# Gates of the first block by seven products of token sums, with one weight sum per attention step

## What is computed

```python
h = rmsnorm(x, norm_attn) * (1 + scale) + shift
qa, ka, va, qb, kb, vb, ga, gb = split(h @ w_in)    # ga, gb: 1024 columns each
ya = gqa_attend(qa, ka, va)                         # 8 heads, 512 wide
yb = rmsnorm(diff_attend(qb, kb, vb, lam), subln)   # 4 heads of 128
merged = sigmoid(ga) * (ya @ w_oa) + sigmoid(gb) * (yb @ w_ob)
x = x + g_a * (merged @ w_out)
x = x + g_m * moe(modulated rmsnorm(x))             # 32 experts, 4 per token
```

## Time and profile before

| | us |
|---|---|
| median of 3 runs | 1747.19 (1745.96 to 1748.6) |
| profiled execution | 1749.62 |
| its span | 1747.8 |
| PE busy | 1635.1 (94%) |
| DVE, ACT busy | 730.3 (42%), 277.9 (16%) |
| mean granted clock of PE | 0.99 |

### The profile page before, as it was taken

How to read it: one execution, slowest core, us unless ns; L and a number is a source line. 1 busy time by engine, 2 the same in 40 slices (tenths; PEclk the granted TensorE clock), 3 DMA queues, 4 the chain that set the end, 5 groups by cost and what they waited for, 6 DMA issues and landing times.

```text
span 1747.8 us, 18802 instructions
## 1 busy us (share of the span) xinstructions
PE 1635.1 (94%) x7152; PEld 873.7 (50%) x7152; DVE 730.3 (42%) x1327; ACT 277.9 (16%) x611; POOL 25.1 (1%) x30
## 2 busy tenths in 40 slices
PE   5999999999989798898897988998999999999998
PEld 3567786533333242333332423333686776688754
DVE  2796432333314223233142233233234663677755
ACT  3123440301010010100100100000243333010000
POOL 0210000000000000000000000000000000000000
PEclk9999999999999999999999999999999999999999
DMA  9796236899999999999999999999733334454440
GB/s 381 277 338 192 94 112 238 336 429 429 429 430 429 429 431 428 430 430 429 431 429 429 431 428 430 431 427 421 257 110 131 114 141 144 145 188 150 158 179 24
DMA packets 86685, 537.18 MB, mean 307 GB/s; under 512 B 6208, under 2 KB 7616, under 8 KB 60512
## 3 DMA queue, kind: packets, MB, share of 16 engines
q1 hardware_dynamic: 82816, 530.60, 74.8%
q10 hardware_dynamic: 3808, 5.78, 0.9%
HBM read 535.31 MB, written 1.05 MB: 307 GB/s over the span
## 4 chain that ended last, share of the span: by engine, by line
PE 67%; DMA 25%; DVE 5%; DVEq 1%; issue 1%; POOL 0%; ACT 0%; SPq 0%; POOLq 0%
PE ps L2398 22%; PE ps L1986 21%; DMA ring<-in_w_up 14%; DMA ring<-in_w_gate 10%; PE ps L2750 6%; PE ps L2980 4%; PE ps L2368 3%; PE ps L2460 2%; DVE arena L1167 2%; DMA ring<-in_w_ada 2%; PE ps L2865 1%; PE ps L2972 1%; PE ps L2249 1%; PE ps L2200 0%; PE ps L2196 0%
## 5 line engine op out<-in xcount | busy, mean ns | idle before, releaser
L2398 PE MATMUL ps<-ring,arena 128*64 128x512 f32 x2288 | 513.5, 597 | 51.5 <-DMA ring<-in_w_gate 23.1
L2398 PEld LDWEIGHTS ps<-ring,arena 128*64 128x64 f32 x2288 | 160.8, 137 | 386.1 <-issue 314.5
L2398 PE MATMUL ps<-arena 128*64 128x512 f32 x784 | 178.8, 601 | 10.1 <-DMA arena<-in_w_up 5.6
L1986 PE MATMUL ps<-ring,arena 128*128 128x512 f32 (+1 forms) x528 | 183.1, 502 | 0.3 <-issue 0.3
L1986 PE MATMUL ps<-arena,ring 128*128 128x256 f32 x704 | 158.2, 382 | 0.3 <-ACT arena L805 0.3
L1986 PEld LDWEIGHTS ps<-arena,ring 128*128 128x128 f32 x704 | 131.9, 190 | 28.2 <-issue 6.8
L1986 PEld LDWEIGHTS ps<-ring,arena 128*128 128x128 f32 x528 | 99.3, 190 | 74.5 <-issue 68.1
L877 ACT ACTIVATE arena<-ps 128x512 f32<-128x512 f32 x32 | 19.1, 597 | 670.6 <-PE ps L2438 670.6
L2398 PEld LDWEIGHTS ps<-arena 128*64 128x64 f32 x784 | 56.1, 138 | 117.8 <-issue 101.8
L1457 DVE TENSOR_TENSOR arena<-ps,arena 128x512 f32<-128x512 f32 x32 | 22.1, 692 | 202.2 <-PE ps L2398 202.2
L1482 DVE TENSOR_TENSOR arena<-ps,g_moe 64x512 f32<-64x512 f32 x32 | 21.9, 683 | 185.6 <-PE ps L2398 185.6
(11 more groups left out here) (361 smaller groups left out, 1591.1 us busy)
## 6 DMA issues: line engine op xcount, KB each, us to landing
ring<-in_w_up SPq DMA_DIRECT2D x54, 2048.0 KB, 33.8
ring<-in_w_down SPq DMA_DIRECT2D x53, 2048.0 KB, 31.8
ring<-in_w_gate SPq DMA_DIRECT2D x47, 2048.0 KB, 33.6
ring<-in_w_in SPq DMA_DIRECT2D x23, 2048.0 KB, 9.1
arena<-in_w_down SPq DMA_DIRECT2D x17, 2048.0 KB, 32.0
arena<-in_w_up SPq DMA_DIRECT2D x16, 2048.0 KB, 30.5
arena<-in_w_gate SPq DMA_DIRECT2D x15, 2048.0 KB, 30.8
ring<-in_w_ada SPq DMA_DIRECT2D x12, 2048.0 KB, 17.3
```

The costliest lines, as they stand in the source:

```text
L1986: last = pe.matmul(dst, a, b, start=k == 0, stop=k == len(terms) - 1)
L2398: mm = pe.matmul(dst[CAP * g:CAP * g + CAP, :], stationary(half, c), w[:, c, 512 * g:512 * g + 512], start=half == 0 and c == 0, stop=half ...
```

## The change

- **Gates.** Each gate block `u` (0 to 3, 512 columns) is made by seven products of four 128x256 multiplies (`gate_product`), with tokens stationary and weight blocks or their sums moving; 28 products instead of 16 halves of eight. The token sums are those of the value projection, which keep their place; the transposed probabilities move to another for that. Products 1, 6, 5, 3 go to bank 7 and are copied by ACT, 256 columns each (16 copies instead of 8 of 512). 2, 7, 4 go to bank 5, and DVE adds each (`gate_add`, 12 adds).
- **Weight sums.** DVE makes four per block (`gate_sum`), at most one per step. The first stands between the last two value adds, before the loop. One of their two places is the stretch of `const` where the routing constants stood; their load (576 KB) moves from the start of ACT's program to behind the loop.
- **Transposes.** Bank 5 being taken, all go to bank 4, and those of step k wait for ACT's copy of step k - 1.
- **Merge.** Gates are now token by column. So `branch_product` has tokens stationary (32 multiplies of 512 columns), `merged` is token by column, and PE transposes it (`merged_turn`, twice eight pieces), ACT copying the result to `mergedT` in four pieces.
- **Sigmoids.** Four of 1024 columns instead of eight of 512.
- **Router weights.** The eight small loads by ACT stand one per step in steps 17 to 24, instead of two per step in 18 to 21, and their place in memory is another.

```diff
@@ -202,9 +203,38 @@
             return k if k < 16 else 16 + 2 * (k - 16)
-        def gate_fill(k):
-            return 8 + k - 16 if 16 <= k < 24 else k // 2 if k < 16 and k % 2 == 0 else None
+        GATE_FILL = {0: ((0, 1), (0, 2)), 2: ((0, 7),), 3: ((0, 6),), 4: ((0, 5),), 5: ((0, 3),), 6: ((0, 4),),
...
+        GATE_MADE = [g for k in sorted(GATE_FILL) for g in GATE_FILL[k]]
+        GATE_SUMS = {1: (0, 1), 2: (0, 2), 3: (0, 4), 5: (1, 3), 6: (1, 1), 7: (1, 2), 9: (1, 4), 11: (2, 3), 12: (2, 1),
...
+        GATE_ADDS = {1: (0, 2), 5: (0, 7), 7: (0, 4), 9: (1, 2), 12: (1, 7), 14: (1, 4), 16: (2, 2), 18: (2, 7), 19: (2, 4),
...
+        gate_t2 = const[:, P:P + 1024].rearrange("p (j c) -> p j c", j=4)
+        gate_t3 = area(20480, 1024).rearrange("p (j c) -> p j c", j=4)
+        def gate_quarter(u, n):
+            tile, half = {1: (0, 0), 2: (0, 0), 6: (1, 0), 4: (1, 0), 5: (1, 1), 7: (1, 1), 3: (0, 1)}[n]
+            return sig[:, u, tile, T * half:T * half + T]
...
...
@@ -699,7 +729,6 @@
...
                                    bias=modT[:, j, m:m + 1]).then_inc(sem("ht_act"), 1)
-            act.dma_start(const[:, P:C_ROPEC], t["const"][:, P:C_ROPEC]).then_inc(sem("const_in"), 16)
...
@@ -799,28 +828,38 @@
...
                     pt_out(k)
-                if gate_fill(k) is not None and gate_fill(k) % 2 == 1:
-                    s = gate_fill(k) // 2
-                    act.wait_ge(sem("gate_done"), s + 1)
-                    act.activation(sig[:, s, :], bank(7), ACT.Copy).then_inc(sem("gate_read"), 1)
+                for u, n in GATE_FILL.get(k, ()):
+                    if n in (1, 6, 5, 3):
+                        act.wait_ge(sem("gate_done"), gate_number(u, n))
+                        if k == 16:
+                            act.wait_ge(sem("pv_done"), 4)
+                        act.activation(gate_quarter(u, n), bank(7, T), ACT.Copy).then_inc(sem("gate_read"), 1)
...
                     pv_out(4 + k - 1 - 16)
-                if 18 <= k < 22:
-                    a = k - 18
-                    for h in range(2):
+                if 17 <= k < 25:
+                    a = (k - 17) // 2
+                    for h in ((k - 17) % 2,):
...
                                       ).then_inc(sem("rw_in"), 16)
+            act.dma_start(const[:, P:C_ROPEC], t["const"][:, P:C_ROPEC]).then_inc(sem("const_in"), 16)
             act.drain()
-            for s in range(8):
-                act.activation(sig[:, s, :], sig[:, s, :], ACT.Sigmoid).then_inc(sem("sig_ready"), 1)
+            for u in range(4):
+                g = sig[:, u].rearrange("p t n -> p (t n)")
+                act.wait_ge(sem("vb_added"), gate_added(u, 4))
+                act.activation(g, g, ACT.Sigmoid).then_inc(sem("sig_ready"), 1)
...
                                scale=sub08).then_inc(sem("ybt_read"), 1)
+            for q in range(4):
+                tt, half = q // 2, q % 2
+                act.wait_ge(sem("ybt_done"), 2 + q + 1)
+                act.activation(mergedT[:, 4 * half:4 * half + 4, P * tt:P * tt + P],
+                               bank(4 + q).rearrange("p (j q) -> p j q", j=4), ACT.Copy).then_inc(sem("ybt_read"), 1)
...
@@ -1241,6 +1280,30 @@
...
                 dve.tensor_tensor(a, bank(2 * m + 1, T), a, ALU.add).then_inc(sem("vb_added"), 1)
+            def gate_sum(u, n):
+                w = wq_view(W_GATE + u)
+                b11, b12, b21, b22 = w[:, 0:4, 0:T], w[:, 0:4, T:2 * T], w[:, 4:8, 0:T], w[:, 4:8, T:2 * T]
+                if n == 3:
+                    i = W_GATE + u
+                    dve.wait_ge(loaded[i % RING], 16 * (i // RING + 1))
+                    if u:
+                        dve.wait_ge(sem("gate_done"), gate_number(u - 1, 7))
+                    else:
+                        dve.wait_ge(sem("qkt_done"), 12)
+                if n == 4:
+                    dve.wait_ge(sem("gate_done"), gate_number(u, 2))
...
+                a, b, c = {3: (gate_t3, b22, b12), 1: (b12, b12, b11), 2: (gate_t2, b22, b12), 4: (b21, b21, gate_t2)}[n]
+                dve.tensor_tensor(a, b, c, ALU.subtract).then_inc(sem("vb_sums"), 1)
+            def gate_add(u, n):
+                dve.wait_ge(sem("gate_done"), gate_number(u, n))
+                dve.wait_ge(sem("gate_read"), gate_copied(u, {2: 1, 7: 5, 4: 6}[n]))
+                a = gate_quarter(u, n)
+                dve.tensor_tensor(a, bank(5, T), a, ALU.add).then_inc(sem("vb_added"), 1)
...
@@ -1272,8 +1334,9 @@
...
             modulation_out(9)
-            for n, m in VB_SUMS[4:6]:
-                vb_add(n, m)
+            vb_add(*VB_SUMS[4])
+            gate_sum(0, 3)
+            vb_add(*VB_SUMS[5])
...
@@ -1324,22 +1387,30 @@
...
                     step_maxes(k + 2)
+                if k < 16 and k in GATE_ADDS:
+                    gate_add(*GATE_ADDS[k])
+                if k in GATE_SUMS:
+                    gate_sum(*GATE_SUMS[k])
+                if k >= 16 and k in GATE_ADDS:
+                    gate_add(*GATE_ADDS[k])
...
             dve.tensor_tensor(obuf, obuf, brs.unsqueeze(2).broadcast_to([P, 8, P]), ALU.mult).then_inc(sem("on_done"), 1)
+            def merged_part(s):
+                return merged[:, s // 2, 512 * (s % 2):512 * (s % 2) + 512]
             for s in range(4):
...
                 dve.wait_ge(sem("ta_done"), s + 1)
-                dve.tensor_tensor(mergedT[:, 2 * s:2 * s + 2, :].rearrange("p j q -> p (j q)"), bank(s),
-                                  sig[:, s, :], ALU.mult).then_inc(sem("ta_read"), 1)
+                dve.tensor_tensor(merged_part(s), bank(s), sig[:, s % 2, s // 2], ALU.mult).then_inc(sem("ta_read"), 1)
             for s in range(4):
...
-                m = mergedT[:, 2 * s:2 * s + 2, :].rearrange("p j q -> p (j q)")
...
+                m = merged_part(s)
...
@@ -2173,18 +2245,37 @@
...
                     qk_transpose(s - 2)
-            def gate_half(h):
-                s, c = h // 2, h % 2
-                i, c0 = W_GATE + s // 2, T * (s % 2) + P * c
-                if c == 0 and s:
-                    pe.wait_ge(sem("gate_read"), s)
-                ready(i)
-                w = wq_view(i)
-                last = product(bank(7)[:, T * c:T * c + T], [(w[:, j, c0:c0 + P], hT[:, j, 0:T]) for j in range(KC)])
-                if h % 4 == 3:
+            def gate_product(u, n):
+                w = wq_view(W_GATE + u)
+                b11, b12, b21, b22 = w[:, 0:4, 0:T], w[:, 0:4, T:2 * T], w[:, 4:8, 0:T], w[:, 4:8, T:2 * T]
+                j0, tile, source = {1: (0, 0, None), 2: (4, 0, None), 3: (4, 1, 3), 4: (4, 1, None),
+                                    5: (0, 1, 0), 6: (0, 0, 1), 7: (0, 0, 2)}[n]
+                b = {1: b11, 2: b21, 3: b22, 4: b21, 5: b12, 6: gate_t2, 7: gate_t3}[n]
+                a = hT[:, j0:j0 + 4, P * tile:P * tile + P] if source is None else vb_tokens[0][:, source]
+                if n == 1:
+                    ready(W_GATE + u)
+                    if u:
+                        pe.wait_ge(sem("gate_read"), gate_copied(u - 1, 3))
+                elif n == 2:
+                    if u:
+                        pe.wait_ge(sem("vb_added"), gate_added(u - 1, 4))
+                    else:
+                        pe.wait_ge(sem("modt_read"), part(11))
+                elif n in (6, 5, 3):
+                    pe.wait_ge(sem("gate_read"), gate_copied(u, {6: 1, 5: 6, 3: 5}[n]))
+                    pe.wait_ge(sem("vb_sums"), gate_summed(u, 2))
+                else:
+                    pe.wait_ge(sem("vb_added"), gate_added(u, {7: 2, 4: 7}[n]))
+                    pe.wait_ge(sem("vb_sums"), gate_summed(u, {7: 3, 4: 4}[n]))
+                for j in range(4):
+                    last = pe.matmul(bank(5 if n in (2, 7, 4) else 7, T), a[:, j, :], b[:, j, :],
+                                     start=n in (1, 2, 7) and j == 0, stop=j == 3, skip_group_check=n not in (1, 2, 7))
+                    if j == 0:
+                        tell_used(last)
+                last.then_inc(sem("gate_done"), 1)
+                if n == 4:
                     used()
-                if c == 1:
-                    last.then_inc(sem("gate_done"), 1)
...
@@ -2231,23 +2322,24 @@
...
             for k in range(24 + 1):
+                fill = GATE_FILL.get(k, ())
                 if k == 16:
-                    gate_half(gate_fill(k))
+                    gate_product(*fill[0])
+                    fill = fill[1:]
...
                     issued += 2
-                if k != 16 and gate_fill(k) is not None:
-                    gate_half(gate_fill(k))
+                for u, n in fill:
+                    gate_product(u, n)
...
                     pe.wait_ge(sem("pn_done"), k + 1)
-                    if k < 2:
-                        pe.wait_ge(sem("modt_read"), part(10 + k))
-                    if k >= 2:
-                        pe.wait_ge(sem("pt_read"), k - 1)
+                    if k == 0:
```

(28 more changed lines are left out.)

33 lines of the change are left out of this document (22 added, 11 removed), and 3 rows, old and new, of the table GATE_FILL.

## The result

The changed kernel takes **1750.74 us** (median of 15 runs, 1747.59 to 1754.12); the kernel before takes 1747.45 (15 runs, 1745.96 to 1750.21). The ratio is 1.0018, with a 95% interval of 1.0011 to 1.0024: slower by 3.3 us, where 2.0 us faster was forecast. The number lies in the forecast range and within the 0.2% called "the same", but the interval excludes no change, and the sign is the wrong one. The profiled execution took 1748.67 us (span 1746.9).

The account below looks back on a forecast made before the run. PE's own work bounds the first block, whose shift carries to the end: -6.3 + 1.8 + 0.85 + 1.35 + 0.5 - 0.2 = -2.0 us on 1747.2 gives 1745.2 us, range 1741.8 to 1751.

Parts of the forecast that it names:

- The step that failed: First block to kernel end: PE time gained or lost there moves the expert weight stream's start and the end one to one.
- rival 2: First block's gates: DVE becomes the pacer, some 11 products wait 0.75 each, +8.3, total +6.3, 1753.5 us; chance 0.14.
- the 0.03 of rival 2 beside its 0.11: DVE's weight sums: 0.03 for a variant concerning a flush between sums back to back, added to 0.11 for DVE pacing PE.
- the shift at the experts' start is not the shift at the end: One of the prediction's signs of being wrong; it expected experts 2 us earlier and all distances unchanged from there.
- Products for halves: PE in first-block attention: 28 gate products at 1.805 us, 50.5, replace 16 halves, 56.8; gain 6.3 us.
- Step 1: First-block attention: no gate product hides the wait for ACT's copy from the single transpose bank; 0.85 us lost.
- Step 15: First-block attention: without a gate product, PE waits for DVE's normalising; 1.35 us lost.
- Steps 22 and 23: End of first-block attention: ACT's shorter copy wins 0.2 at step 22; PE's wait for a copy loses 0.4 to 0.5 at 23.
- Merge turned back: After the gates: two groups of eight PE transposes turn the merge back, all on the path; 1.8 us lost.
- Clock drop at 306 to 314: Small router products before the experts: granted clock 0.79; more such slow small pieces, 8 us, would lose 1.7 us.
- rival 3: First-block PE: changing over costs 0.15 a product with all stalls, +0.6, or the clock drops, 1.7 lost; about 1748; chance 0.17.
- Constants moved: 576 KB of constants load after the attention instead of at the start: at most 1.5 us gained there, taken as 0.

Follow-up runs that it names:

- with 236 instructions: Changed kernel plus 236 never executed PE instructions in the jumped-over code for further expert passes: 1748.80 us, ratio 1.0003 to the kernel before.
- with 144: Changed kernel plus 144 never executed PE instructions in the jumped-over code for further expert passes: 1746.28 us, ratio 0.9993 to the kernel before.
- with 12: Changed kernel plus 12 never executed PE instructions in the jumped-over code for further expert passes: 1752.45 us, ratio 1.0026 to the kernel before.
- with 24: Changed kernel plus 24 never executed PE instructions in the jumped-over code for further expert passes: 1746.19 us, ratio 0.9992 to the kernel before.
- 144 + 112 = 256: Kernel before plus 112 never executed PE instructions, placing its code behind the branch as in the changed kernel: 1752.81 us, ratio 1.0028.

## Why the prediction was wrong, point by point

**The step that failed** is "what the first block gains or loses moves the start of that stream, and the end of the kernel with it, one to one", repeated at the end as "from there all distances are as before". It took the way from the experts' start to the end as fixed. For data and loads that holds up to 1193 us, where the issues keep their 5.49 us. It left out, and so put at nothing, that removing instructions moves all code behind them. That costs 3.8 us (1750.12 against 1746.28, two kernels that differ only by never executed instructions), and it turns a gain into a loss of 3.3. No rival had this mechanism; rival 2, the slower one, did not come true: PE waits for a DVE result twice in that block, 2.1 us in all, not at each of 11 products. For the 0.03 of rival 2 beside its 0.11 no run shows a cause: in the profile after, the weight sum of 150.55 is 1.22 us long and DVE's next instruction starts at 151.70, 1.15 after the sum's start; behind the sum of 153.34 it is 1.14. The last sentence of the prediction named the sign by which it would be wrong, "the shift at the experts' start is not the shift at the end", and that is what happened.

**With the stop taken out, the total agrees within the noise.** The two kernels with the code at the same place differ by -2.7 us with the stop in both (1750.12 and 1752.81) and by -1.1 and -1.35 with it in neither (1746.28 and 1746.19, against 1747.35 and 1747.54); -2.0 was forecast, and the intervals reach some 1.6 us to either side. The experts' start moves 2.86 in the profiles. Part of this may be lost again while the stream of weights is the limit: the table has 20.48 and 21.87 in place of 20.02, with PE waiting for weights. But over the whole way from the first expert multiply to the second block, executions without a stop take 909.4 to 911.7 us, and this spread hides it.

That the total agrees is in part luck. Of the 2.86, 1.2 are the clock drop that vanished, which the prediction did not count on; without it 1.7 is left. A wait of 0.86 that it missed is in part made up by terms that it set too dear.

Term by term, at the experts' start:

- **Products for halves**: forecast -6.3. Added up start to start over both profiles, waits left out, the 16 halves take 56.8 us and the 28 products 50.4 (1.83 each behind scores, 1.73 behind transposes, 3.55 for two in a row): -6.4. The cost and the mechanism are right. The attention's other PE rows grow by 0.6 in all, which the sum did not have.
- **Step 1**, one bank: forecast 0.85, measured 0.78. **Step 15**: 1.35, measured 1.22. Both mechanisms and sizes right.
- **Step 3**: not forecast, 0.86. The second weight sum, 1.23 us long, stands behind the maximum of the next step on DVE, and the product needs it. With that sum moved to step 1 the wait is gone; with only the product of step 1 moved it stays. The prediction costed a pair of steps in the steady state and not the first, where the chain of sums starts from nothing.
- **Steps 22 and 23**: -0.2 and +0.5 forecast. The product of step 22 starts 1.57 after the transposes of step 21, against 1.78 before: -0.2, right, and the marked wait of 0.28 is gone. The product of step 23 starts 4.96 after them where 5.3 was forecast and PE was to come at 4.9: about 0.1 in place of 0.5. The exponentials start 2.60 behind these transposes, not 2.85; and 2.85 with two exponentials of 0.7 is 4.25, not the 4.4 of the prediction.
- **Merge turned back**: forecast +1.8. The transposes are there (278.52 to 279.39, 0.87 for eight), and the tail without its clock drop grows by 73.48 - (73.06 - 1.19) = +1.6. The 1.19 is the price of the drop in changed code; that it is the same in the kernel before is taken, not shown.
- **Clock drop at 306 to 314**: the prediction had it only as something that might get worse (rival 3). It went away in this profile, as in eight others of ten of changed code: -1.2. That small pieces bring it is not shown: the twelve transposes behind the router products take 2.69 us before (309.70, clock 0.79) and 1.51 after (305.26), the same pieces with the clock at 1.00.
- **Constants moved**: 0 at the start, right; the first gate product starts at 144.7 to 145.2 in all profiles with the clock at 1.00 at 28 to 50 us, before and after.

By these -6.4 + 0.6 + 0.78 + 0.86 + 1.22 - 0.28 + 1.6 - 1.2 = -2.8, the 2.86 measured within rounding. The sum has to close, since the 0.6 (it holds the 0.1 of step 23) and the 1.6 are what is left over of the two stages.

**The range** held the number by luck: its upper end, 1751, is the foot of a rival that did not happen.

## What to carry to other kernels

When a change alters how many instructions PE has ahead of a taken branch, the code behind the branch lands elsewhere in its pieces, and in this kernel the place alone is worth 2.5 to 6.3 us (1748.80 with 236 instructions against 1746.28 with 144, 1752.45 with 12 against 1746.19 with 24), though nothing that runs behind it is touched. Look in the timeline for a stop inside a row of like instructions, released by "issue", behind a branch (here it begins 1.1 to 4.5 us after the first matmul behind it); then put never executed instructions into the part that is jumped over, and compare two kernels only with this settled. The lead at the start of the expert stream, 5.5 us in the first pair of profiles, was still whole in the load at 1193 us (5.49); the last 0.8 us gained there, by two sums at step 1, became a wait of 0.96 for weights in its profile.

## What the runs showed of the hardware

- The queue taken to be that of PE's instructions brings packets of 16 KB (38 packets, 0.62 MB in the page after). Behind the one branch studied here the next piece is there 5.5 to 5.8 us after PE starts on the first; PE stopped 4.48, 3.2 to 3.5, 1.13 and 0 us with 8, 20, 40 and 132 instructions left in the first, by the count of the table. The places of the stops repeat after 256 instructions: 144 + 112 = 256 put the stop back behind the ninth matmul. With half of that, the run with 144 would have had 4 left and stopped about two matmuls in; it has no stop. At the branch itself a packet at 1201.0 comes ahead of the first matmul behind it at 1203.99, with 1.27 us of idle time.
- A stop in PE cost more than its length here: from the branch to the second block 6.6 us are lost for one of 3.15, with the granted clock at 0.50 for the 6 us behind it in that profile, and 3.8 for one of 3.20 where the clock stayed at 1.00.
- Two drops of the granted clock (28 to 50 us: 0.84; 304 to 314: 0.83) come and go between executions and shift all that follows, by 2.5 and 1.2 us. The first comes with either kernel; the second was in all three profiles of the kernel before and in one of ten of changed code. Here a landmark of one profile was only comparable with one of another where both show the same clock ahead of it.
